# First norm's shift by TensorE, scale and shift chunks in turn, first query chunk in steps of two feature tiles

## What is computed

```python
c_act = jax.nn.silu(c)                                   # c: 1 x 1024
mod = c_act @ w_ada[l] + b_ada[l]                        # 1024 -> 6 x 1024
sh_m, sc_m, gt_m, sh_f, sc_f, gt_f = jnp.split(mod, 6, axis=-1)
h = modulate(rms_norm(x, g_mix[l]), sh_m, sc_m)          # norm * (1 + sc_m) + sh_m
proj = jnp.einsum('bsd,de->bse', h, w_in[l])             # then q, k, v of two attentions, gates
```

## Time and profile before

| What | Value |
|---|---|
| Median of 3 runs | 893.09 us (893.0 to 893.72) |
| Profiled execution, its own time | 895.13 us |
| Span of that execution | 893.3 us |
| Mean granted TensorE clock | 0.96 |
| PE busy | 800.7 us, 90% of the span |
| DVE busy | 690.2 us, 77% |
| ACT busy | 459.9 us, 51% |
| Weight chunks loaded | 141 of 1 MB |

### The profile page before, as it was taken

How to read it: one execution, slowest core, us unless ns; L and a number is a source line. 1 busy time by engine, 2 the same in 40 slices (tenths; PEclk the granted TensorE clock), 3 DMA queues, 4 the chain that set the end, 5 groups by cost and what they waited for, 6 DMA issues and landing times.

```text
span 893.3 us, 13849 instructions
## 1 busy us (share of the span) xinstructions
PE 800.7 (90%) x5400; PEld 723.8 (81%) x5400; DVE 690.2 (77%) x910; ACT 459.9 (51%) x629; POOL 159.4 (18%) x109
## 2 busy tenths in 40 slices
PE   0599999998978999999997899679969979999986
PEld 0499988777977999999997788568837869999985
DVE  4964587787857899999995799999957838596652
ACT  2544368667526645454544646664462265255641
POOL 0000021231000122113211019975410000000000
PEclk9799999999988999999998899889979999999998
DMA  9977696754643466576674061111211714273101
GB/s 353 394 278 265 233 327 246 283 194 177 230 148 142 165 254 240 207 267 240 226 252 172 0 236 48 47 48 51 91 48 60 290 48 145 101 274 132 59 2 47
DMA packets 26043, 156.73 MB, mean 175 GB/s; under 512 B 2659, under 2 KB 7052, under 8 KB 7820
## 3 DMA queue, kind: packets, MB, share of 16 engines
q1 hardware_dynamic: 21360, 148.91, 45.6%
q10 hardware_dynamic: 4636, 7.18, 2.6%
HBM read 155.01 MB, written 1.06 MB: 175 GB/s over the span
## 4 chain that ended last, share of the span: by engine, by line
PE 52%; DVE 28%; issue 10%; ACT 6%; DVEq 1%; ACTq 1%; DMA 1%; POOL 0%; POOLq 0%
PE wide L1170 20%; PE bank L1170 19%; DVE w_lo L772 10%; DVE arena L1012 6%; DVE w_lo L802 4%; DVE arena L938 2%; PE bank L1398 2%; ACT w_hi L364 1%; DVE att L833 1%; PE wide L1540 1%; PE bank L1516 1%; DMA raw<-in_w 1%; PE bank L1528 1%; PE wide L1258 1%; DVE h_lo L838 1%
## 5 line engine op out<-in xcount | busy, mean ns | idle before, releaser
L802 DVE TENSOR_TENSOR w_lo<-raw,w_hi 128x2048 fp32r<-128x2048 f32 x93 | 218.9, 2355 | 55.0 <-ACT w_hi L364 52.5
L1170 PE MATMUL bank<-h_hi,w_hi 128*128 128x256 f32 x736 | 214.8, 292 | 20.0 <-DVE h_lo L838 12.9
L1170 PE MATMUL bank<-h_lo,w_hi 128*128 128x256 f32 x736 | 211.8, 288 | 0.0
L1170 PE MATMUL bank<-h_hi,w_lo 128*128 128x256 f32 x736 | 211.6, 287 | 0.0
L1170 PE MATMUL wide<-h_hi,w_hi 128*128 128x256 f32 (+1 forms) x528 | 181.6, 344 | 30.6 <-DVE w_lo L802 13.6
L364 ACT CAST w_hi<-raw 128x2048 fp32r<-128x2048 f32 x93 | 177.6, 1910 | 47.0 <-PE bank L1170 18.9
L1170 PE MATMUL wide<-h_lo,w_hi 128*128 128x256 f32 (+1 forms) x528 | 177.2, 336 | 0.0
L1170 PE MATMUL wide<-h_hi,w_lo 128*128 128x256 f32 (+1 forms) x528 | 176.8, 335 | 0.0
L1170 PEld LDWEIGHTS bank<-h_hi,w_hi 128*128 128x128 f32 x736 | 144.6, 196 | 22.2 <-issue 13.9
L1170 PEld LDWEIGHTS bank<-h_lo,w_hi 128*128 128x128 f32 x736 | 145.2, 197 | 0.0
L1170 PEld LDWEIGHTS bank<-h_hi,w_lo 128*128 128x128 f32 x736 | 144.8, 197 | 0.0
(11 more groups left out here) (244 smaller groups left out, 1107.4 us busy)
## 6 DMA issues: line engine op xcount, KB each, us to landing
raw<-in_w SPq DMA_DIRECT2D x141, 1024.0 KB, 4.9
xs<-in_xs ACTq DMA_DIRECT2D x2, 1024.0 KB, 12.9
consts<-diff ACTq DMA_DIRECT2D x8, 128.0 KB, 6.6
cond<-in_cond ACTq DMA_DIRECT2D x1, 1024.0 KB, 7.1
out<-xs SPq DMA_DIRECT2D x2, 512.0 KB, 3.0
consts<-in_c ACTq DMA_DIRECT2D x1, 576.0 KB, 3.8
arena<-in_cond ACTq DMA_DIRECT2D x1, 512.0 KB, 7.1
consts<-in_c ACTq DMA_DIRECT2D x1, 512.0 KB, 3.4
```

The costliest lines, as they stand in the source:

```text
L802: nc.vector.tensor_tensor(w_lo[:, slot, :], raw[:, rslot, :], w_hi[:, slot, :].bitcast(F32), ALU.subtract).then_inc(sem("lo_done"), 1)
L1170: last = mm(out, w[a], x[b], start=start and n == 0, stop=stop and n == 2, skip_group_check=skip)
```

## The change

The shift's four chunks get a kind of their own, "shift". They hold the matrix untransposed, and TensorE multiplies them with the condition vector laid down a column (`cond_col`, 128 x 8): sixteen float32 matmuls with one moving column for each chunk (`shift_matvec`). `cond_col` comes with `vec` and gets its Silu on ACT. The chunks now alternate: lin 0, shift 0, mod 0, shift 1, mod 1, shift 2, mod 2, shift 3, mod 3. VectorE finishes two feature tiles after each mod chunk, and TensorE takes these two tiles of the first query chunk (`first_chunk`). ACT issues `xs` first and `rel` and `onehot` last, and stores the relative bias after `rstd`. The `trev` loads go behind the cast of lin 1.

```diff
-MOD_FIRST = 8
-N_MOD = 48
+MOD_FIRST = 4
+HEAD = 2 * MOD_FIRST
+N_MOD = 44
...
 def stream_order():
-    order = [("lin", 0)] + [("mod", m) for m in range(MOD_FIRST)]
+    order = [("lin", 0)]
+    for m in range(MOD_FIRST):
+        order += [("shift", m), ("mod", m)]
...
-                    sp.wait_ge(sem("lo_done" if freed[0] == "lin" else "mod_done"), freed[1] + 1)
+                    sp.wait_ge(sem({"lin": "lo_done", "mod": "mod_done", "shift": "shift_done"}[freed[0]]), freed[1] + 1)
...
             me = Steps(act, "act_steps")
+            act.dma_start(xs[:, :, 0:T], xs_d[:, :, 0:T]).then_inc(sem("x_loaded"), 16)
             act.dma_start(cond_ada, bass.AP(cond_d.tensor, 0, [[0, P], [1, D]])).then_inc(sem("cond_ada_loaded"), 16)
+            act.dma_start(vec[:, :], vec_d).then_inc(sem("vec_loaded"), 16)
+            act.dma_start(c0[:, :], c0_d).then_inc(sem("c0_loaded"), 16)
             act.dma_start(rel[0:32, :], rel_d).then_inc(sem("rel_loaded"), 16)
             act.dma_start(onehot, c1_d[0:33, 1152:1536]).then_inc(sem("rel_loaded"), 16)
-            act.dma_start(xs[:, :, 0:T], xs_d[:, :, 0:T]).then_inc(sem("x_loaded"), 16)
-            act.dma_start(c0[:, :], c0_d).then_inc(sem("c0_loaded"), 16)
-            act.dma_start(vec[:, :], vec_d).then_inc(sem("vec_loaded"), 16)
...
             nc.scalar.activation(cond_ada, cond_ada, ACT.Silu).then_inc(sem("cond_ada_ready"), 1)
+            act.wait_ge(sem("vec_loaded"), 16)
+            nc.scalar.activation(cond_col[:, :], vec[:, VEC["cond_col"]:VEC["cond_col"] + 8], ACT.Silu).then_inc(sem("cond_col_ready"), 1)
             split(0)
+            act.wait_ge(sem("eps_set"), 2)
+            squares("mix", lambda k: [("x_loaded", 16)] if k == 0 else [])
+            rstd_of("mix")
             act.wait_ge(sem("bias_row"), 1)
             nc.scalar.copy(urow, bank[3][0:8, 0:384]).then_inc(sem("bias_row_out"), 1)
             act.wait_ge(sem("bias_row_out"), 1)
             act.dma_start(diff_d, urow).then_inc(sem("bias_stored"), 16)
+            shift_hi("mix")
+
+            act.dma_start(consts[:, 0:1152], c1_d[:, 0:1152]).then_inc(sem("c1_loaded"), 16)
+            split(1)
             act.wait_ge(sem("bias_stored"), 16)
...
             for h in range(TREV):
                 load_trev(h)
-            act.wait_ge(sem("eps_set"), 2)
-            squares("mix", lambda k: [("x_loaded", 16)] if k == 0 else [])
-            rstd_of("mix")
-            shift_hi("mix")
-
-            act.dma_start(consts[:, 0:1152], c1_d[:, 0:1152]).then_inc(sem("c1_loaded"), 16)
-            split(1)
...
             dve.wait_ge(sem("cond_ada_ready"), 1)
+            dve.wait_ge(sem("vec_loaded"), 16)
             for m in range(MOD_FIRST):
                 mod(m, RAW_OF_MOD[m] % RAW, 16 * (RAW_OF_MOD[m] // RAW + 1), 1, 1)
-            dve.wait_ge(sem("vec_loaded"), 16)
-            mod_bias(0, 8)
-            coefficients(0, "g_mix", mod_row(ADA_SC_M, 0))
-            norm("mix", 1)
...
+                dve.wait_ge(sem("shift_done"), m + 1)
+                nc.vector.tensor_tensor(shift_m[:, 2 * m:2 * m + 2], wide[:, m, 0:2],
...
+                if m == 0:
+                    dve.wait_ge(sem("rstd_ready"), 1)
...
+                for k in (2 * m, 2 * m + 1):
+                    nc.vector.scalar_tensor_tensor(norm_tmp[:, k, :], xs[:, k, 0:T], coef[:, k:k + 1], rstd[:, 0:T],
+                                                   ALU.mult, ALU.mult).then_inc(sem("normed"), 1)
+                for k in (2 * m, 2 * m + 1):
+                    dve.wait_ge(sem("shift_m"), m + 1)
+                    dve.wait_ge(sem("norm_hi"), k + 1)
+                    nc.vector.scalar_tensor_tensor(h_lo[:, k, 0:T], norm_tmp[:, k, :], shift_m[:, k:k + 1],
+                                                   h_hi[:, k, 0:T].bitcast(F32), ALU.add, ALU.subtract).then_inc(sem("norm_lo"), 1)
             split(1)
...
+            pe.wait_ge(sem("c0_loaded"), 16)
+            sum_squares("mix")
             pe.wait_ge(sem("rel_loaded"), 32)
             pe.wait_ge(sem("rel_one"), 1)
             mm(bank[3][0:8, 0:384], rel[:, :], onehot, start=True, stop=True).then_inc(sem("bias_row"), 1)
-            pe.wait_ge(sem("c0_loaded"), 16)
-            sum_squares("mix")
+            def shift_matvec(m):
+                r = RAW_OF_SHIFT[m]
+                pe.wait_ge(sem(f"arrived{r % RAW}"), 16 * (r // RAW + 1))
+                pe.wait_ge(sem("cond_col_ready"), 1)
+                for t in range(2):
+                    for k in range(KT):
+                        last = mm(wide[:, m, t:t + 1], raw[:, r % RAW, 256 * k + P * t:256 * k + P * (t + 1)],
+                                  cond_col[:, k:k + 1], start=(k == 0), stop=(k == KT - 1))
+                last.then_inc(sem("shift_done"), 1)
+            def first_chunk(k0):
+                pe.wait_ge(sem("lo_done"), 1)
+                for k in (k0, k0 + 1):
+                    tile_ready("mix")(k)
+                    for m in range(2):
+                        last = triple(halves(bank[0])[m], whl(0, 256 * k + P * m, P), hhl(k, 0, T), k == 0 and m == 0,
+                                      k == KT - 1, skip=True)
+                if k0 == KT - 2:
+                    last.then_inc(sem("lin_done"), 1)
+            shift_matvec(0)
+            for m in range(1, MOD_FIRST):
+                shift_matvec(m)
+                first_chunk(2 * m - 2)
+            first_chunk(KT - 2)
```

More of the change, by code:

```diff
@@ L40 @@
 W_PAIRS = 8
-MOD_FIRST = 8
-N_MOD = 48
+MOD_FIRST = 4
+HEAD = 2 * MOD_FIRST
+N_MOD = 44
 LIN_OPEN = 1
-ADA_SC_M, ADA_SH_M, ADA_GT_M, ADA_SH_F, ADA_SC_F, ADA_GT_F = 0, 4, 8, 12, 16, 20
-E_SC, E_SH, E_GT, O_SC, O_SH, O_GT = 24, 28, 32, 36, 40, 44
+ADA_SC_M, ADA_GT_M, ADA_SH_F, ADA_SC_F, ADA_GT_F = 0, 4, 8, 12, 16
+E_SC, E_SH, E_GT, O_SC, O_SH, O_GT = 20, 24, 28, 32, 36, 40
 CONV_W = 31
@@ L85 @@
 RAW_OF_MOD = [0] * N_MOD
+RAW_OF_SHIFT = [0] * MOD_FIRST
 for _r, (_kind, _n) in enumerate(ORDER):
-    (RAW_OF_LIN if _kind == "lin" else RAW_OF_MOD)[_n] = _r
+    {"lin": RAW_OF_LIN, "mod": RAW_OF_MOD, "shift": RAW_OF_SHIFT}[_kind][_n] = _r
 VEC_SIZES = [("mod_bias", 4 * N_MOD), ("g_mix", 8), ("g_ffn", 8), ("g_final", 8),
@@ L139, in build @@
         small = sb("small", [P, 64])
+        shift_m = sb("shift_m", [P, 8])
+        cond_col = sb("cond_col", [P, 8])
         zeros = sb("zeros", [P, 512], BF16)
@@ L219, in conv_part, with norm_shift @@
             return acc, src
+        def norm_shift(sh, k, v):
+            return shift_m[:, k:k + 1] if sh is None else shift_col(sh, k, v)
         def mod_row(base, v):
@@ L269, in load @@
                 if freed is not None:
-                    sp.wait_ge(sem("lo_done" if freed[0] == "lin" else "mod_done"), freed[1] + 1)
+                    sp.wait_ge(sem({"lin": "lo_done", "mod": "mod_done", "shift": "shift_done"}[freed[0]]), freed[1] + 1)
                 src = w_d[bass.ds(r, 1), :, :].rearrange("a p n -> (a p) n")
                 sp.dma_start(raw[:, slot, :], src).then_inc(sem(f"arrived{slot}"), 16)
-            for r in range(MOD_FIRST + 4):
+            for r in range(HEAD + 4):
                 load(r, r % RAW, ORDER[r - RAW] if r >= RAW else None)
@@ L279, in _ @@
                 for n in range(4):
-                    load(4 * i + MOD_FIRST + 4 + n, n, ("lin", 3 * i + n) if n < 3 else ("mod", i + MOD_FIRST))
+                    load(4 * i + HEAD + 4 + n, n, ("lin", 3 * i + n) if n < 3 else ("mod", i + MOD_FIRST))
             r0 = RAW_OF_LIN[LIN_FFN]
@@ L398, in shift_hi @@
                     nc.scalar.activation(h_hi[:, k, s * T:(s + 1) * T], norm_tmp[:, k, :], ACT.Identity,
-                                         bias=shift_col(sh, k, v), scale=1.0).then_inc(sem("norm_hi"), 1)
+                                         bias=norm_shift(sh, k, v), scale=1.0).then_inc(sem("norm_hi"), 1)
             eps_col = small[:, 63:64]
@@ L779, in mods_before @@
                 r, mods = RAW_OF_LIN[j] - 1, []
-                while r > MOD_FIRST and ORDER[r][0] == "mod":
+                while r > HEAD and ORDER[r][0] == "mod":
                     mods.insert(0, ORDER[r][1])
@@ L857, in _ @@
                     j = 6 * i + n + 2
-                    r = MOD_FIRST + 4 * ((n + 2) // 3) + (n + 2) % 3
+                    r = HEAD + 4 * ((n + 2) // 3) + (n + 2) % 3
                     m = None
@@ L963, in _ @@
             me.leave(FF_STEPS - 1)
-            mod_bias(20, 24)
-            mod_bias(24, 36)
+            mod_bias(16, 20)
+            mod_bias(20, 32)
             coefficients(16, "e_norm", mod_row(E_SC, 0))
@@ L1148, in _ @@
             split(LIN_OOUT + 3)
-            mod_bias(44, 48)
+            mod_bias(40, 44)
             for i in range(4):
@@ L1234, in _ @@
             for i in range(2):
-                for n in range(6):
+                for n in range(0 if i else 1, 6):
                     qkv_step(i, n)
@@ L1704 @@
```

(10 more changed lines are left out.)

29 lines of the change are left out of this document (22 added, 7 removed).

## The result

The changed kernel takes 911.56 us (median of 4 runs, 906.87 to 914.75) against 893.4 us for the kernel before in the same runs. The ratio is 1.0198 with a 95% interval of 1.0149 to 1.0247. It is slower by 18.2 us. The forecast was 904.0 us with a range of 897 to 916; the time of the first rival, products at the slow clock, was 914.5.

A forecast was written before the change was run, and what follows sets the result against it. Bound: the head's weight-chunk loads and VectorE's work on them, before unbroken TensorE work. Lin 1 8.9 us later plus 2.0 for a slow start makes 10.9 us, on the median 904.0 us; range 897 to 916.

The forecast's parts named there:

- the first rival: Shift products on TensorE run at the slow clock, 6.8 us a chunk; lin 1 at 64.8, time 914.5 us; chance 0.28.
- the forecast case: Program head: condition vector late, shift products at the fast clock; 904.0 us, own range 899 to 907; chance 0.52.
- the last mod chunk near 46 us: Sign of being right, in the weight loads: the last mod chunk lands at 45.8 us instead of 33.0.
- its sign of being wrong: Wide Silu at 10 us, DMA share 1.0 until 40 us, or one-column matmuls more than 110 ns apart.
- The late condition vector: ACT's first loads: with xs in front, the condition lands at 18.3 us instead of 7.9, delaying the fifth weight request.
- Turns by the packet: First loads: SP's and ACT's queues alternate packet by packet, 368 against 423 packets from 8 to 15.5 us before.
- The price of a shift chunk: TensorE: 32 weight loads of 107 ns at the fast clock, 3.4 us a chunk; 6.8 us at the slow clock.
- 2.0 us for a slow start of lin 1: Lin 1's first matmuls: a slow clock for 5.4 us would lose 2.7 us, otherwise nothing; 2.0 taken.
- The tail of 8.8 to 8.9 us behind the last mod chunk: From the last mod chunk's landing to lin 1: mod, two tiles, cast and subtraction, 8.8 to 8.9 us instead of 12.9.
- The faster rival: Head: early condition and nearly free shift products, 890.2 us, chance 0.07; with 3.4 us a chunk 893.7, no change, 0.06.
- Nothing for `trev` and the later bias rows: trev loads delay only lin 2's cast, by 1.3 us under lin 1's matmuls; bias rows needed at 110 us: no cost.
- everything behind lin 1 moves with it one for one: Behind the head both programs hold the same work in the same order, so lin 1's delay passes fully into the time.

The follow-up runs named there:

- e4: The kernel before, with only ACT's first loads in the order of the changed kernel (xs first): 901.78 us, ratio 1.0090.
- e1: The changed kernel with ACT's first loads reordered, condition vector and vec ahead of xs: 907.67 us, ratio 1.0164.
- e2: The changed kernel with each one-column shift product streaming the same column 128 times, same result and weight loads: 901.23 us, ratio 1.0084.
- e5: The changed kernel with the edits of e1 and e2 together: 901.78 us, ratio 1.0074.
- e7: The kernel of e6, with VectorE taking mod chunks 0, 1 and 2 before it waits for rstd: 895.23 us, ratio 1.0006.
- e6: The kernel of e5, with shift chunks 0 and 1 before the sums of squares in TensorE's queue: 900.70 us, ratio 1.0064.
- e8: The kernel before, with scale and shift chunks alternating and tiles made in pairs, both chunk kinds staying on VectorE: 907.03 us, ratio 1.0144.
- e3: The changed kernel with 4 of the 16 products of each shift chunk, so another output: 901.27 us, ratio 1.0088.
- e11: The kernel of e7 with the changed kernel's one-column shift products in place of the 128-column ones: 900.20 us, ratio 1.0073.

## Why the prediction came out as it did

The forecast's sign was right, and the time fell into the range of 897 to 916 us. But it missed the forecast case's own range, 899 to 907 us, and of that case only the first half happened. Of the signs that the prediction names, those of the late condition came true; the last mod chunk near 46 us, lin 1 at 54 to 55 us and a slow clock in lin 1 did not, and its sign of being wrong, one-column matmuls more than 110 ns apart, did: they came 207 ns apart.

- **The late condition vector: right.** Forecast 18.3 us, measured 17.86 (start of the Silu); the fifth weight chunk was requested at 23.1 us (forecast 23.8), and the transfers stood at 0.00 from 19 to 24 us. e4 prices this one edit at 8.2 us in the kernel before. In the changed kernel mending it alone gives 3.9 us (e1), because the sums of squares then wait for `xs`.
- **Turns by the packet: not borne out as one to one.** From 8 to 15.5 us ACT's queue moved 716 packets to SP's 322, where before it was 423 to 368. With `xs` first, ACT's queue got more than two packets for one of SP's; in e1 it was 360 to 357. No run shows why. The condition vector came 0.5 us earlier than forecast, so little hung on it.
- **The price of a shift chunk: wrong, and the failing term of the sum.** I took 3.4 us by the fast clock. Shift 2 and 3 took 6.62 us each, the two before them 11.90 together. The forecast put the loads at the fast clock "because the clock is high after the sums". It was high until 32 us, two microseconds into the shift chunks, and then fell while TensorE issued without a pause. The argument against the rival, that TensorE is not still, was true and did not help. The slow price in the prediction, 6.8 us, was within 3%. The rival's chain came out almost as written: shift 3 forecast to end at 58.5, measured 60.8; lin 1 forecast 64.8, measured 66.7.
- **Why a miss of 12.0 us at lin 1 is one of 7.6 us in the time: in part luck.** Lin 1 came at 66.70 us where the forecast had 54.7. Against that stand the 2.0 us for a slow start of lin 1, which did not come, and 1.2 us less behind it; the profiled execution is thus 8.8 us over the forecast's 906.0. The median lies 3.2 us below the profiled execution, where the forecast took 2.0. Nothing in the forecast's argument led to these three. The rival's 914.5 us also holds 2.5 us of a slow start that did not happen.
- **The same term at the fast clock: right.** e2 makes the forecast's condition true. Its shift 0 ends at 32.8 us (forecast 33.0), its last weight chunk lands at 46.1 (45.8), its lin 1 starts at 54.58 (54.7). Its time of 901.23 us is 7.6 us over before; the forecast without its 2.0 us for a slow start of lin 1, which e2 doesn't have, is 902.0. The fast pace also cost a little more than taken: 3.78 us a chunk, 118 ns a load, against 3.4 us and 107 ns.
- **2.0 us for a slow start of lin 1: wrong for the changed kernel.** Lin 1 began at 66.70 us and ran at full clock (44 matmuls in the stretch below). It does occur elsewhere: 1.7 us in e5 and in e7, 1.4 us in e6.

```profile
66.70:72.00 5.30, 5.30 (x44) 5.30 (x45) 4.44 (x5) 2.04 (x2) 0.00 (x0) 1.00 0.90 311
```

- **The tail of 8.8 to 8.9 us behind the last mod chunk: right.** In e2 it is 54.58 - 46.1 = 8.4 us. That two tiles at a time shorten the tail was right too, but e8 shows the price that this has where the first pair waits for `rstd`. In the changed kernel that wait was hidden behind the one for shift 0; in e6 it came out.
- **The faster rival needed an early condition and nearly free products.** e5 is near its first half: condition early, a shift chunk 3.78 us. The rival had 893.7 us for that, measured 901.78. It had the sums at 20.9 us, because I let them follow the cast; but they wait for `xs`, which is there at 18.9 us, so they ended at 26.2. I had not carried over that `xs` lands at 18.3 us even when it isn't first. This error didn't touch the forecast, in which `xs` is first.
- **Nothing for `trev` and the later bias rows: not contradicted in the changed kernel.** Neither the `trev` loads nor the copy and store of the bias rows are in its chain; the product with `rel` is, with 0.74 us ahead of shift 0, for which the forecast's sum had 0.6. The copy and store on ACT, now between `rstd` and the first tiles, do stand in the chain where shift 0 no longer hides them, with some 0.7 us together in e3 and in e6.

Put together: of the 18.2 us, 10.3 go when the shift's products run at the fast clock (e2). The other 7.6 us went only when three more repairs had been added to it one after another: the condition first (e5), two shift chunks ahead of the sums (e6), and VectorE's mod chunks ahead of its wait for `rstd` (e7). Each repair uncovered the next wait.

That everything behind lin 1 moves with it one for one holds within 3 us. From lin 1's start to the end of the span the profiled executions took 844.3 to 847.5 us in ten kernels, and 848.9, 848.7 and 851.4 in e5, e7 and e6, the three whose lin 1 began slow. By the granted clock of those traces the slow stretches there add up to 59 to 61 us in the ten, to 68 in e5 and e7 and to 74 in e6.

What stays open is what decides where the clock falls and when it rises again. It is also open where the other runs of the changed kernel, up to 8 us below the profiled one, gained their time; their mean granted clocks are higher, but only the profiled execution has a trace.

## What to carry to other kernels

Moving work to an engine that looks idle moves it in front of what is queued there, and here also in front of the requests for data: the first release of a buffer by TensorE stood behind sums that waited for the activations. A matrix-vector product on TensorE pays for its weight loads, and here it paid nearly twice (6.62 us for 32 loads instead of 3.78), because the clock fell under one-column products; streaming the same column 128 times took no longer at the same clock and kept it high. A forecast should price such products at the slow clock unless a row shows them at the fast one. The order of the first small transfers is worth checking before anything else, since in e4 a transfer of 1 MB in 1 KB rows in front of one of 0.5 MB cost 8 us on its own.

## What the runs showed of the hardware that was not expected

- TensorE was busy 30.00 of 30 us, from 34 to 64 us, and was granted 0.50 of its clock, the level of 1.2 GHz, throughout. Before the clock fell, at 32 us, it had issued the sums of 256 columns and then, for 2 us, weight loads with one-column matmuls, and nothing else until 42 us. With 128 columns behind the same loads (e2) it was granted 1.00, 2.4 GHz, from 28 us to the start of lin 1 and beyond. The Trainium skill ("TensorE: Matmul & The Clock Gate", section "Part 1: The HAM clock gate") says that the gate follows how busy TensorE has been lately. The trace agrees with this only if busy is something else than the profile's busy column: by that one both kernels are at 100% (from 34 to 64 us in the changed kernel, from 28.3 to 36.4 us in e2), and their clocks are 0.50 and 1.00.
- The column of the granted clock reads 1.00 in the first 30 us of these traces even where the loads last 333 to 337 ns, the duration of the slow stretches (in e11 from 13.5 to 27 us). Early in the program the durations decide.
- A load of 128 float32 columns came every 207 ns at the slow clock (6.62 us for 32) and every 118 ns in e2 (3.78 us for 32). By the formula of the Trainium skill ("TensorE: Matmul & The Clock Gate", section "LDWEIGHTS") a load of 128 columns takes an estimated 107 ns. The fast clock is 10% above that and the slow one nearly twice.
- Kernels that hold the same work from lin 1 on can differ by microseconds behind it: e6 took 2.5 us longer than e2 in a single gate product at 118 us, at a place that no edit touches.
